# A chunked gated recurrence in a two-layer backbone step: forward and backward keys in one operand per level, the diagonal first, and the output-gate weighting behind the levels

## The chip, the cores and the metric

One core of a Trainium2 chip runs the whole step in one launch. The metric is the device time of an execution in microseconds (us). All arithmetic is in fp32. Engines are named as in the profile: PE (TensorE), DVE (VectorE), ACT (ScalarE), POOL (GpSimd), SP (the queue that issues the weight loads).

## The reference, cut to what matters

Two layers (L = 0, 1) over 384 tokens: 128 context tokens and 256 latent ones. Each layer mixes tokens (attention beside a bidirectional gated recurrence, joined by sigmoid gates) and then applies a mixture of 16 experts. The recurrence is the part that the change touches:

```
def hgrn_chunk_scan(q, k, v, log_f, s0):
    ...
        bcum = jnp.cumsum(gc, axis=2)
        o_inter = jnp.einsum('bhck,bhkv->bhcv', qc * jnp.exp(bcum), state)
        diff = bcum[:, :, :, None, :] - bcum[:, :, None, :, :]
        decay = jnp.exp(jnp.where(incl, diff, -jnp.inf))
        scores = jnp.einsum('bhtk,bhsk,bhtsk->bhts', qc, kc, decay)
        o_intra = jnp.einsum('bhts,bhsv->bhtv', scores, vc)
...
    o_f, s_f = hgrn_chunk_scan(q, k_f, v, lf_f, s0_f)
    o_b, s_b = hgrn_chunk_scan(flip(q), flip(k_b), flip(v), flip(lf_b), s0_b)
    o = o_f + flip(o_b)
    o = rms_norm(o, hnorm_w) * jax.nn.silu(heads(h_g.astype(F32), HGRN_V))
```

There are 4 heads of width 128. For a query t and a key s the score is a sum over channels of q, k and the decay between s and t: with the forward keys for s before t, with the backward keys for s after t, and with both on the diagonal.

## The kernel before

**Tiling.** Tokens lie in 3 tiles of 128; with 4 heads that makes 12 segments, and one operand of the recurrence is 128 channels x 1536 (12 x 128) values. `qh` holds q, `kg[0]` and `kg[1]` the forward and backward keys, `Cs[0]` and `Cs[1]` the running sums of the log forget gates (all in the buffer `gen`). The 128 x 128 score matrices of the 12 segments are gathered in `AT`.

**Levels.** A score matrix is filled level by level: with block size m = 64, 32, ..., 1 the pairs (s, t) that lie in the two halves of one block of 2m are computed, with the decay measured from the block's middle. The old order has 15 steps: each of the 7 levels once forward and once backward (step 2k and 2k+1), then the diagonal. For a step, POOL writes differences of `Cs` to the middle (L628, L629: two instructions of 128x768 each), ACT takes the exponential in place (L760, 128x1536), DVE multiplies one half of each block by keys and the other by queries (L1012, two instructions of 128x768) into `W[s % 2]`, and PE multiplies that operand with itself (L1470: 3 tiles x 4 heads, 128x128 each; the profile records two entries per fp32 matmul, so a step is 24). DVE copies each tile's result into `AT` where the step's mask is set (L1025, 3 instructions). `E[0]`, `E[1]`, `W[0]` lie in the buffer `ring`, `W[1]` in `modb`. The exponents use `E[s % 2]`, and POOL may write them for step s once DVE has made the operand of step s-2 (`lv_W`).

**Order of the work.** Each engine follows one hand-written program, and semaphores join them. PE writes projections into two banks in turn (`group` counts them). In the stretch at issue its program is: the 8 gate groups `ga` (L1410, 8 matmuls of 128x384 each), behind each one step of the levels (`LEV_AT`); in layer 0 then 8 modulation units `mod` 12 to 19 (L1364 and L1368, in pairs, each pair followed by two sums L1376), with a step behind each of the first 7; in layer 1 the last 7 steps with nothing between; then the branch groups `wba` (L1410 with 4 matmuls). Between these stand the key transposes `kd` (L1331), the chunk states (L1601) and the outputs (L1611 to L1616). ACT evacuates `ga` with a sigmoid (L815) and must load a function table on each change between sigmoid and exponential. For the modulation units it copies (L697, L702) and stores to memory (L706), and a pair may only be copied once the pair before it is stored.

**Behind the levels.** Four operands are exponentials of `Cs`, multiplied by `fin` (L1035): `W[1]` and `W[0]` by q for the outputs, `E[0]` and `E[1]` by the keys for the states. POOL makes two differences for them (L636, 128x1536). DVE copies the transposed keys (L1039), makes the states (L1136, L1141) and then norms the outputs. POOL multiplies the output gate `sg` by the norm's weights (L616, 3 instructions) ahead of its first difference.

**Weight loads.** SP loads 2 MB units into a ring of 4 slots in the order of use (L466). A unit's load is issued when the last group of the unit 4 places ahead of it is done: `mod` 15 when `ga` 7 is done, `mod` 16 to 19 when `mod` 12 to 15 are, and the branch weights `wba` when `mod` 16 is. The three expert weights (2 MB each) of an expert come through 6 slots behind `x_mid` and the last groups of the mixer.

## Time and profile before

| | us |
|---|---|
| median of 3 runs | 1647.63 |
| the runs | 1644.11 to 1647.88 |
| span of the profiled execution, first to last instruction | 1645.4 |
| PE busy | 1449.9 (88% of the span) |
| DVE busy | 533.4 (32%) |
| ACT busy | 340.7 (21%) |
| POOL busy | 212.7 (13%) |

The profile gives the execution's span; its time with what lies around it is not listed apart from the three runs. The span is 2.2 us below their median and within their range. PE's busy share is an average: in layer 0 the levels of the recurrence run from 275 to 381 us of the span, in layer 1 from 1061 to 1148 us. The experts fill 571 to 850 and 1325 to 1621 us.

### The profile page before, as it was taken

The numbers are of one execution on the slowest core, as the hardware profiler recorded it, in microseconds if no ns is written. First come the engines' busy times: TensorE is split into PE (matmuls) and PEld (weight loads), VectorE is DVE, ScalarE is ACT, GpSimd is POOL, SyncE is SP. The second block draws the span as 40 slices with busy tenths as digits, with TensorE's granted clock in tenths as the row PEclk, the third lists the DMA queues.
The fourth block names the chain that finished last, engine by engine and source line by source line (L and its number), as shares of the span: only waits on it lengthen the run. The fifth ranks groups of instructions, "written<-read, shape, count | busy, mean of one in ns | idle before, by whom it ended". The sixth has DMA issues, their size and how long they took to land.

```text
span 1645.4 us, 19345 instructions
## 1 busy us (share of the span) xinstructions
PE 1449.9 (88%) x7515; PEld 813.0 (49%) x7516; DVE 533.4 (32%) x1097; ACT 340.7 (21%) x499; POOL 212.7 (13%) x213
## 2 busy tenths in 40 slices
PE   4699998999999799989965999898999688999882
PEld 1365545766654354444423654577654344454441
DVE  1333323564212511121125353348511432111113
ACT  1105533532100201100101174354100100011100
POOL 2160004321100100000012500444100000000001
PEclk9799999999999799999987999999999889999997
DMA  9635552185333999996984412211223544799994
GB/s 347 237 106 186 186 215 80 52 292 182 128 107 113 397 349 396 397 344 248 399 305 141 155 54 70 84 52 52 90 103 111 221 158 169 278 398 394 398 394 184
DMA packets 157047, 352.48 MB, mean 214 GB/s; under 512 B 5880, under 2 KB 13128, under 8 KB 156992
## 3 DMA queue, kind: packets, MB, share of 16 engines
q1 hardware_dynamic: 138208, 314.48, 51.7%
q0 software_dynamic: 6576, 23.26, 3.9%
q10 hardware_dynamic: 12208, 13.98, 2.6%
q8 instruction: 38, 0.62, 0.2%
q14 instruction: 17, 0.14, 0.0%
HBM read 336.15 MB, written 15.55 MB: 214 GB/s over the span
## 4 chain that ended last, share of the span: by engine, by line
PE 74%; DVE 8%; SPq 7%; DMA 4%; issue 4%; ACT 1%; POOL 1%; DVEq 0%; ACTq 0%; POOLq 0%
PE pG L1410 22%; PE pS L1490 10%; PE pG L1402 8%; SPq L475 6%; PE pG L1505 5%; PE pG L1639 5%; PE pG L1498 4%; PE pS L1470 2%; PE pG L1364 2%; PE pX L1470 2%; DMA ring<-in_w_mod_dram 2%; PE pX L1331 2%; PE pX L1490 2%; DMA ring<-in_w_exp_up_dram 1%; PE pG L1376 1%
## 5 line engine op out<-in xcount | busy, mean ns | idle before, releaser
L1410 PE MATMUL pG<-hT,ring 128*128 128x384 f32 x896 | 299.7, 489 | 1.6 <-ACT gen L849 1.6
L1490 PE MATMUL pS<-ring,gen 128*64 128x256 f32 x2048 | 230.6, 381 | 12.2 <-DMA ring<-in_w_exp_up_dram 9.8
L1410 PEld LDWEIGHTS pG<-hT,ring 128*128 128x128 f32 x896 | 168.1, 191 | 115.6 <-issue 4.8
L1490 PEld LDWEIGHTS pS<-ring,gen 128*64 128x64 f32 x2048 | 149.5, 138 | 100.5 <-issue 20.1
L1402 PE MATMUL pG<-ring,hT 128*128 128x512 f32 (+1 forms) x384 | 150.0, 548 | 1.4 <-issue 0.7
L1505 PE MATMUL pG<-ring,gen 128*64 128x512 f32 x512 | 116.9, 598 | 5.1 <-DVE gen L1287 5.1
L1282 DVE TENSOR_TENSOR gen<-pS,gen 128x256 f32<-128x256 f32 x32 | 13.6, 424 | 314.8 <-PE pS L1490 314.8
L1402 PEld LDWEIGHTS pG<-ring,hT 128*128 128x128 f32 x384 | 72.6, 192 | 72.1 <-issue 67.7
L1498 PE MATMUL pG<-hrow,gen 128*64 128x512 f32 x408 | 96.0, 604 | 2.2 <-DVE gen L1182 1.5
L662 POOL DMA_INDIRECT gen<-y_scr,idx x12 | 11.6, 963 | 630.1 <-ACTq L899 627.0
L878 ACT COPY gen<-pG 128x512 f32<-128x512 f32 x32 | 18.8, 586 | 349.1 <-PE pG L1505 349.1
L1639 PE MATMUL pG<-ring,hrow 128*128 128x512 f32 x192 | 82.9, 593 | 2.5 <-DVE hrow L1167 2.5
L553 POOL TENSOR_TENSOR stat<-stat,half 128x8 f32<-128x8 f32 (+3 forms) x22 | 23.9, 1086 | 336.2 <-DVE stat L962 260.3
L1505 PEld LDWEIGHTS pG<-ring,gen 128*64 128x64 f32 x512 | 33.9, 136 | 67.5 <-issue 54.8
L1364 PE MATMUL pG<-ring,cst 128*32 128x512 f32 x384 | 52.6, 660 | 14.2 <-DMA ring<-in_w_mod_dram 14.2
L1639 PEld LDWEIGHTS pG<-ring,hrow 128*128 128x128 f32 x192 | 36.3, 190 | 48.7 <-issue 45.0
L1331 PE MATMUL pX<-const,gen 128*128 128x128 f32 x224 | 40.7, 291 | 22.3 <-DVE gen L1284 13.6
L1331 PEld LDWEIGHTS pX<-const,gen 128*128 128x128 f32 x224 | 23.2, 141 | 63.2 <-issue 26.0
L1498 PEld LDWEIGHTS pG<-hrow,gen 128*64 128x64 f32 x408 | 30.4, 140 | 48.2 <-issue 42.1
L628 POOL TENSOR_TENSOR ring<-gen 128x768 f32<-128x768 f32 x28 | 43.4, 1549 | 82.5 <-DVE modb L1012 41.9
L1331 PE MATMUL pS<-const,hrow 128*128 128x128 f32 x32 | 7.0, 391 | 47.0 <-DVE hrow L968 47.0
L1410 PE MATMUL pG<-modb,ring 128*128 128x384 f32 x128 | 46.7, 519 | 0.0
(269 smaller groups left out, 1713.4 us busy)
## 6 DMA issues: line engine op xcount, KB each, us to landing
ring<-in_w_exp_up_dram SPq DMA_DIRECT2D x32, 2048.0 KB, 20.7
ring<-in_w_exp_down_dram SPq DMA_DIRECT2D x32, 2048.0 KB, 19.3
ring<-in_w_exp_gate_dram SPq DMA_DIRECT2D x32, 2048.0 KB, 18.3
ring<-in_w_mod_dram SPq DMA_DIRECT2D x24, 2048.0 KB, 9.0
ring<-in_w_in_dram SPq DMA_DIRECT2D x20, 2048.0 KB, 7.8
modb<-mod_scr POOLq DMA_DIRECT2D x20, 512.0 KB, 8.9
y_scr<-gen ACTq DMA_DIRECT2D x72, 128.0 KB, 5.5
ring<-in_w_out_dram SPq DMA_DIRECT2D x4, 2048.0 KB, 10.2
```

What stands on the lines that cost most here:

```text
L475: return sp.dma_start(dst, src).then_inc(landed[s0 + part], 16)
L553: return pool.tensor_tensor(stat[:, stat0:stat0 + width], stat[:, stat0:stat0 + width], half[:, 0:width], ALU.pow).then_inc(done, 1)
L628: pool.tensor_tensor(out[:, :, :, 0, :], mid, base[:, :, :, 0, :], ALU.subtract)
L1331: return pe.transpose(out, in_, ident[0:n, 0:n])
L1364: pe.matmul(ps[32 * q:32 * q + 32, :], cst[:, 2 * q + k, :, :].rearrange("p c r -> p (c r)"), w[:, 2 * q + k, :], start=(k == 0), stop=(k ...
L1402: ins = pe.matmul(ps[:, 0:width], hT[:, k, t * P:(t + 1) * P], w[:, k, 0:width], start=(k == 0), stop=(k == KC - 1))
L1410: ins = pe.matmul(ps[:, 0:TOK], w[:, k, c0:c0 + P], src[:, k, :], start=(k == 0), stop=(k == nk - 1))
L1470: ins = pe.matmul(bank[2 + u % 4][:, P * h:P * (h + 1)], lhs, rhs, start=True, stop=True)
L1490: ins = pe.matmul(dst[64 * hf:64 * hf + 64, 0:256], x[:, k, :], w[:, k, 256 * hf:256 * (hf + 1)], start=(k == 0), stop=(k == KC - 1))
L1498: ins = pe.matmul(dst[64 * hf:64 * hf + 64, :], sel1[:, t, :], hrow[:, t, 512 * hf:512 * (hf + 1)], start=(t == 0), stop=(t == NT - 1))
L1505: ins = pe.matmul(dst[64 * hf:64 * hf + 64, :], x[:, k, :], w[:, k, 512 * hf:512 * (hf + 1)], start=(k == 0), stop=(k == 3))
L1639: ins = pe.matmul(ps, mergedT[:, k, t * P:(t + 1) * P], w[:, k, :], start=(k == 0), stop=(k == KC - 1))
```

## The change

The levels now take 8 steps. Step 0 is the diagonal; steps 1 to 7 are the levels, each once for both directions. Two operands are used per step, in the same four buffers: `LR[s % 2]`, a left and a right one, `E[0]` and `E[1]` for even steps, `W[0]` and `W[1]` for odd ones. The left one holds the keys with their decays (forward keys in the first half of each block, backward keys in the second), the right one the queries with theirs, so that one product yields the forward scores in one corner of a block and the backward scores in the other. POOL now makes four differences per step (two per operand), ACT two exponentials, DVE three products (two of 128x768 for the left operand, one of 128x1536 for the right). PE multiplies left by right, and the masks shrink from 15 to 8. POOL may write the operands of step s once PE has done step s-2 (`lv_mm`), since they are now what PE reads.

All 8 steps stand behind the 8 `ga` groups, in both layers; the modulation units of layer 0 follow without any. The exponentials for `fin` now come ahead of ACT's copies of the modulation units. `fin` 0 and 1 make the keys' operands, `fin` 2 and 3 the outputs', and these two stand behind `wba` 1 on DVE. `kd` 0 to 3 stand together behind `wba` 1 on PE, and DVE's copies of them also wait for the exponentials, which read the buffers that they overwrite. POOL's products of `sg` stand behind its differences.

```diff
-LEV_STEPS = 2 * NLEV + 1
-
-LEV_AT = {g: k for k, g in enumerate([("ga", j) for j in range(KC)] + [("mod", m) for m in range(MOD_LEV, MOD_LATE - 1)])}
+LEV_STEPS = NLEV + 1
...
+        LR = (E, W)
...
+                pool.wait_ge(at_outv, ATT_STEPS * (L + 1))
+                pool.wait_ge(C_ready, 2 * (L + 1))
+                for s in range(1, LEV_STEPS):
+                    m = 64 >> (s - 1)
+                    if s >= 2:
+                        pool.wait_ge(lv_mm, LEV_TILES * L + NT * (s - 1))
...
+                    left, right = (x.rearrange("p (s b u m) -> p s b u m", s=SEG, u=2, m=m) for x in LR[s % 2])
+                    pool.tensor_tensor(left[:, :, :, 0, :], mid[0], base[0][:, :, :, 0, :], ALU.subtract)
+                    pool.tensor_tensor(left[:, :, :, 1, :], base[1][:, :, :, 1, :], mid[1], ALU.subtract).then_inc(lv_D, 1)
+                    pool.tensor_tensor(right[:, :, :, 0, :], mid[1], base[1][:, :, :, 0, :], ALU.subtract)
+                    pool.tensor_tensor(right[:, :, :, 1, :], base[0][:, :, :, 1, :], mid[0], ALU.subtract).then_inc(lv_D, 1)
+
+                for d, dst in ((0, E[0]), (1, W[0])):
+                    pool.wait_ge(lv_mm, LEV_TILES * L + NT * (LEV_STEPS - 1 + d))
...
                 for t in range(NT):
                     pool.wait_ge(sg_mul, NT * L + t + 1)
...
             def lev(L, s):
-                if s < 2 * NLEV:
-                    act.wait_ge(lv_D, 2 * NLEV * L + s + 1)
-                    act.activation(E[s % 2], E[s % 2], ACT.Exp).then_inc(lv_E, 1)
+                if s < LEV_STEPS:
+                    for side in range(2):
+                        act.wait_ge(lv_D, 2 * (NLEV * L + s - 1) + side + 1)
+                        x = LR[s % 2][side]
+                        act.activation(x, x, ACT.Exp).then_inc(lv_E, 1)
...
-                    lev(L, LEV_AT[("ga", j)] + 2)
...
+                    lev(L, j + 1)
...
+                if s == 0:
+                    dve.wait_ge(C_ready, 2 * (L + 1))
+                    dve.tensor_tensor(LR[0][0], kg[0], kg[1], ALU.add).then_inc(lv_W, 1)
+                elif s < LEV_STEPS:
+                    m = 64 >> (s - 1)
+                    left, right = LR[s % 2]
+                    dve.wait_ge(lv_E, 2 * (NLEV * L + s - 1) + 1)
+                    for u in range(2):
+                        x, k = (v.rearrange("p (s b u m) -> p s b u m", s=SEG, u=2, m=m)[:, :, :, u, :]
+                                for v in (left, kg[u]))
+                        dve.tensor_tensor(x, x, k, ALU.mult)
+                    dve.wait_ge(lv_E, 2 * (NLEV * L + s - 1) + 2)
+                    dve.tensor_tensor(right, right, qh, ALU.mult).then_inc(lv_W, 1)
...
-                fin(L, 0, W[1], qh)
+                fin(L, 0, E[1], kg[1])
                 fin(L, 1, E[0], kg[0])
                 wba(L, 0)
...
+                for i in range(4):
+                    kd_evac(L, i)
                 wba(L, 1)
...
+                fin(L, 2, W[1], qh)
+                fin(L, 3, W[0], qh)
                 wba(L, 2)
```

**PE, layer 0, from the last `ga` group on.** 128x384 with x8 is a `ga` group, 128x128 a step, 32x512 x8 with 32x128 x4 a modulation unit, 32x512 x2 the two sums. Before:

```order
L1410 MATMUL pG<-hT,ring 128x384 x8
L1470 MATMUL pS<-modb 128x128 x4
L1470 MATMUL pX<-modb 128x128 x8
L1364 MATMUL pG<-ring,cst 32x512 x8
L1368 MATMUL pG<-brow,const 32x128 x4
L1470 MATMUL pS<-ring 128x128 x8
L1470 MATMUL pX<-ring 128x128 x4
L1364 MATMUL pG<-ring,cst 32x512 x8
L1368 MATMUL pG<-brow,const 32x128 x4
L1470 MATMUL pX<-modb 128x128 x4
L1470 MATMUL pS<-modb 128x128 x8
L1376 MATMUL pG<-modb,const 32x512 x2
```

and with the change:

```order
L1401 MATMUL pG<-hT,ring 128x384 x8
L1461 MATMUL pS<-modb,ring 128x128 x4
L1461 MATMUL pX<-modb,ring 128x128 x8
L1355 MATMUL pG<-ring,cst 32x512 x8
L1359 MATMUL pG<-brow,const 32x128 x4
L1355 MATMUL pG<-ring,cst 32x512 x8
L1359 MATMUL pG<-brow,const 32x128 x4
L1367 MATMUL pG<-modb,const 32x512 x2
```

The seven steps between the modulation units are gone, and the last step stands behind the last `ga` group.

**DVE, both layers, the first steps behind the last product of the output gate.** `modb` or `ring` ahead of the arrow is the operand being made. Before:

```order
L1115 TENSOR_TENSOR ring<-pG,ring 128x512
L1012 TENSOR_TENSOR ring<-gen,ring 128x12x64 x2
L1012 TENSOR_TENSOR modb<-gen,ring 128x12x64 x2
L1025 COPY_PREDICATED ring<-masks,pS 128x4x128 x2
L1025 COPY_PREDICATED ring<-masks,pX 128x4x128
L1012 TENSOR_TENSOR ring<-gen,ring 128x24x32 x2
```

and with the change:

```order
L1108 TENSOR_TENSOR ring<-pG,ring 128x512
L997 TENSOR_TENSOR ring<-gen 128x1536
L1005 TENSOR_TENSOR ring<-ring,gen 128x12x64 x2
L1007 TENSOR_TENSOR modb<-modb,gen 128x1536
L1017 COPY_PREDICATED ring<-masks,pS 128x4x128 x2
L1017 COPY_PREDICATED ring<-masks,pX 128x4x128
L1005 TENSOR_TENSOR ring<-ring,gen 128x24x32 x2
L1007 TENSOR_TENSOR ring<-ring,gen 128x1536
```

The first operand is now the sum of the two keys (L997), which needs no exponential; behind it every step has three products and three masked copies.

**PE behind the levels.** L1331 (now L1322) with x8 are two of the four `kd`, L1601 (now L1584) the states, L1611 (now L1595) the outputs. Before:

```order
L1410 MATMUL pG<-modb,ring 128x384 x4
L1331 MATMUL pS<-const,ring 128x128 x8
L1410 MATMUL pG<-modb,ring 128x384 x4
L1331 MATMUL pX<-const,ring 128x128 x8
L1410 MATMUL pG<-modb,ring 128x384 x4
L1601 MATMUL pS<-gen 128x128 x4
```

and with the change:

```order
L1401 MATMUL pG<-modb,ring 128x384 x8
L1322 MATMUL pS<-const,ring 128x128 x8
L1322 MATMUL pX<-const,ring 128x128 x8
L1401 MATMUL pG<-modb,ring 128x384 x4
L1584 MATMUL pS<-gen 128x128 x4
```

Two branch groups now stand ahead of the first transposes.

## Rows read from the trace of the kernel before

**Rows 1.** the page: chain of waits by engine, share of the span

```profile
PE 74%; DVE 8%; SPq 7%; DMA 4%; issue 4%; ACT 1%; POOL 1%; DVEq 0%; ACTq 0%; POOLq 0%
```

**Rows 2.** chain of waits, layer 0, gate groups and steps (start, us, what)

```profile
289.00 5.16 PE pG L1410 x16
294.17 1.78 PE pX L1470 x16
295.95 0.89 PE pS L1470 x8
296.84 5.16 PE pG L1410 x16
...
333.37 0.89 PE pS L1470 x8
```

**Rows 3.** timeline, layer 0, first step (start, us, instruction, [idle before, releaser])

```profile
265.80 0.69 DVE L1115 TENSOR_TENSOR ring<-pG,ring 128x512 f32<-128x512 f32 x1 [7.25 <-ACT ring L807]
266.57 1.27 POOL L616 TENSOR_TENSOR ring<-ring,hnw 128x512 f32<-128x512 f32 x1 [6.87 <-DVE ring L1115]
...
272.11 1.48 POOL L629 TENSOR_TENSOR ring<-gen 128x768 f32<-128x768 f32 x1
272.33 2.94 DVE L1012 TENSOR_TENSOR ring<-gen,ring 128x768 f32<-128x768 f32 x2 [5.84 <-ACT ring L760]
...
275.33 3.79 PE L1470 MATMUL pS<-ring 128*128 128x128 f32 x16 [5.10 <-DVE ring L1012]
...
276.42 0.49 ACT L815 ACTIVATE hrow<-pG 128x384 f32<-128x384 f32 x1
```

**Rows 4.** lines of the levels: count, ns (min/median/max), starts, form

```profile
L628 POOL TENSOR_TENSOR ring<-gen x28: 1466/1503/2076, 267.8 to 1133.5; 128x768 f32<-128x768 f32 x28
...
L1012 DVE TENSOR_TENSOR ring<-gen,ring x28: 936/951/2090, 272.3 to 1137.2; 128x768 f32<-128x768 f32 x28
...
L1014 DVE TENSOR_TENSOR ring<-gen x2: 1731/1736/1741, 368.2 to 1143.4; 128x1536 f32<-128x1536 f32 x2
...
L1025 DVE COPY_PREDICATED ring<-masks,pS x46: 712/731/746, 278.2 to 1148.2; 128x512 f32<-128x512 uint8 x46
...
L760 ACT ACTIVATE ring<-ring x28: 1467/1485/1490, 270.7 to 1136.5; 128x1536 f32<-128x1536 f32 x28
...
L760 ACT ACT_TABLE_LOAD  x18: 1283/1283/1283, 265.7 to 1119.2; - x18
```

**Rows 5.** chain of waits, layer 1: its first level

```profile
1060.90 3.78 PE pS L1470 x16
```

**Rows 6.** stretches: us, PE PEld DVE ACT POOL busy, clock, DMA share, GB/s

```profile
355.00:365.00 10.00, 10.00 (x80) 6.01 (x73) 5.95 (x8) 3.12 (x4) 0.00 (x0) 1.00 0.98 360
...
1121.00:1148.00 27.00, 20.50 (x172) 19.40 (x171) 26.84 (x33) 8.54 (x8) 11.43 (x7) 1.00 0.17 70
```

**Rows 7.** timeline, layer 1, last levels and what follows them

```profile
1128.72 2.05 PE L1470 MATMUL pX<-ring 128*128 128x128 f32 x16 [1.78 <-DVE ring L1012]
...
1148.01 2.75 PE L1410 MATMUL pG<-modb,ring 128*128 128x384 f32 x8
...
1148.25 2.75 POOL L636 TENSOR_TENSOR ring<-gen 128x1536 f32<-128x1536 f32 x1 [0.25 <-PE pS L1470]
...
1154.33 1.18 PE L1331 MATMUL pS<-const,ring 128*128 128x128 f32 x8 [3.58 <-DVE ring L1035]
...
1155.31 4.39 PE L1410 MATMUL pG<-modb,ring 128*128 128x384 f32 x8
...
1169.15 1.28 PE L1611 MATMUL pX<-gen,ring 128*128 128x128 f32 x10
```

**Rows 8.** DMA issues of 255 to 400 us: count, KB each, median us to landing

```profile
ring<-in_w_mod_dram SPq DMA_DIRECT2D x7, 2048.0 KB, 8.5
```

**Rows 9.** timeline, layer 0: first branch group, first recurrence output

```profile
384.87 2.85 PE L1410 MATMUL pG<-modb,ring 128*128 128x384 f32 x8
...
407.59 1.28 PE L1611 MATMUL pX<-gen,ring 128*128 128x128 f32 x10
```

More of the change, by code:

```diff
@@ L611, in _ @@
                     last.then_inc(qk_ready, 1)
+                pool.wait_ge(at_outv, ATT_STEPS * (L + 1))
[4 more added lines that the diff above has]
+                        pool.wait_ge(lv_mm, LEV_TILES * L + NT * (s - 1))
+                    base, mid = [], []
+                    for d in range(2):
+                        base.append(Cs[d][:, :, 1 - d:129 - d].rearrange("p s (b u m) -> p s b u m", u=2, m=m))
+                        mids = Cs[d][:, :, m:m + 128 - 2 * m + 1:2 * m] if m < 64 else Cs[d][:, :, 64:65]
+                        mid.append(mids.unsqueeze(3).broadcast_to([P, SEG, 64 // m, m]))
+                    left, right = (x.rearrange("p (s b u m) -> p s b u m", s=SEG, u=2, m=m) for x in LR[s % 2])
[5 more added lines that the diff above has]
+                    pool.wait_ge(lv_mm, LEV_TILES * L + NT * (LEV_STEPS - 1 + d))
+                    end = Cs[d][:, :, 128:129].broadcast_to([P, SEG, P])
+                    pool.tensor_tensor(dst.rearrange("p (s t) -> p s t", s=SEG), end, Cs[d][:, :, 1 - d:129 - d],
+                                       ALU.subtract).then_inc(fin_D, 1)
                 for t in range(NT):
@@ L815, in _ @@
                     act.activation(mergedT[:, j, :], ps[:, 0:TOK], ACT.Sigmoid).then_inc(ga_ready, 1)
[L816 to L830 removed]
+                    lev(L, j + 1)
+                act.wait_ge(lv_mm, LEV_TILES * L + NT * (LEV_STEPS - 1))
+                act.activation(E[1].rearrange("p (s t) -> p s t", s=SEG), Cs[1][:, :, 0:128], ACT.Exp)
                 for d in range(2):
@@ L835, in _ @@
                 act.activation(E[0], E[0], ACT.Exp).then_inc(fin_E, 1)
+                act.wait_ge(lv_mm, LEV_TILES * (L + 1))
+                act.activation(W[1].rearrange("p (s t) -> p s t", s=SEG), Cs[0][:, :, 1:129], ACT.Exp).then_inc(fin_E, 1)
                 act.wait_ge(fin_D, 2 * L + 2)
                 act.activation(W[0], W[0], ACT.Exp).then_inc(fin_E, 1)
-                act.wait_ge(lv_W, LEV_STEPS * (L + 1))
-                act.activation(E[1].rearrange("p (s t) -> p s t", s=SEG), Cs[1][:, :, 0:128], ACT.Exp).then_inc(fin_E, 1)
+                if L == 0:
+                    for m in range(MOD_LEV, MOD_LATE, 2):
+                        mod_copy(m)
+                        mod_copy(m + 1)
+                        mod_store(m)
+                        mod_store(m + 1)
                 act.wait_ge(st_ready, 4 * L + 2)
@@ L1574, in _ @@
                     cols(L, ("ga", j), w, P * (j % 4), hT, KC)
-                    lev(L, LEV_AT[("ga", j)])
+                    lev(L, j)
                 if L == 0:
                     for m in range(MOD_LEV, MOD_LATE, 2):
-                        for i in range(2):
-                            mod(m + i)
-                            if ("mod", m + i) in LEV_AT:
-                                lev(L, LEV_AT[("mod", m + i)])
+                        mod(m)
+                        mod(m + 1)
                         mod_sum(m)
                         mod_sum(m + 1)
-                else:
-                    for s in range(KC, LEV_STEPS):
-                        lev(L, s)
                 w = unit_in(L, ("wba", 0))
@@ L1589, in _ @@
                     cols(L, ("wba", j), w, P * j, attnT, 4)
-                    if j == 0:
-                        kd(L, 0)
-                        kd(L, 1)
                     if j == 1:
-                        kd(L, 2)
-                        kd(L, 3)
+                        for i in range(4):
+                            kd(L, i)
                     if j == 2:
```

68 lines of the change are left out of this document (7 added, 61 removed).

## The prediction

> **What bounds the kernel now.** I read the page first: PE is busy for 88% of the span, as the table of the page's shares has it, and the chain of waits lies on PE for 74% [rows 1]. So the question at each place is whether PE waits, and for whom. The levels are then read in the chain of layer 0 [rows 2]: a gate group of 5.16 us and a step of 1.78 + 0.89 = 2.67 us follow each other without a gap, 7.84 us a pair. There PE is the bound, and the other engines' work on a step is hidden. It is not hidden in two places. Before the first step PE is idle for 5.10 us, and then its clock is low: 16 entries take 3.79 us [rows 3]. In layer 1 the last seven steps have no gate group beside them: between 1121 and 1148 us PE is busy for 20.50 of 27.00 us, DVE for 26.84 [rows 6].
>
> **What it removes on PE.** 15 steps become 8: 7 steps of 2.67 us, 18.7 us of PE work per layer and 37.4 in all, if PE were the only bound. POOL, ACT and DVE keep their work on the levels (7 steps with twice as much each instead of 14), save that DVE makes 7 x 3 = 21 fewer masked copies of 0.73 us per layer [rows 4], all off the path.
>
> **A step from now on.** The first four POOL differences of the levels start from 267.8 to 272.11 us, one every 1.44 [rows 3, 4]: 5.8 us in all for a step. ACT needs two exponentials of 1.48 and, around the gate sigmoid of 0.49, two table loads of 1.28 [rows 3, 4]: 6.0 us. DVE needs two products of 0.95 us, one of 1.74 (the sum at L1014 has its shape) and three copies of 0.73: 5.8 us [rows 4]. Each is under PE's 7.84. But POOL and DVE hold each other up. A POOL difference of 1.48 us starts at 272.11 and ends at 273.59; two DVE products, from 272.33 on, take 2.94 instead of 1.9 us, and for 1.26 of these POOL was still busy [rows 3]. The longest of L1012 is 2.09 us and of L628 2.08, where 0.95 and 1.50 are the medians [rows 4], so it goes both ways, and the masked copies, at most 0.75, are spared. The two thus take turns: 5.8 + 2 x 0.95 + 1.74 = **9.4 us** per step, more than PE's 7.84. With steps 1 to 7 that is what sets the pace, and PE waits some 1.6 us in each. The Trainium skill, GPSIMD Engine Reference, section 3.1 on elementwise work, gives about 2.6 cycles per element for a two-input GpSimd operation, 1.66 us for 768 elements; by that the pace would be 10.3 us and the kernel some 11 us slower than I forecast. The trace has 1.47 to 1.50, and I keep that.
>
> **Both layers, start to last step.** I count in the times of layer 0 before. The last gate product of DVE ends at 266.5 [rows 3], and the new first operand is a sum of 1.74 us with no exponential, ready at 268.3. `ga` 0 ends at 275.33 - 5.10 = 270.2. So step 0 runs at once, to 272.9: the 5.1 us and the low clock behind it go. What is late next is step 1. POOL has done it early: moving the output-gate products behind the levels lets it in, and it was idle for 6.87 us before the last of them [rows 3]. But ACT takes its exponentials only behind the sigmoid of `ga` 0: 270.2 + 0.5 + 1.3 + 2 x 1.5 = 275. POOL's four differences for step 2 start at 272.9, and DVE's three products, from 273.6 on, take turns with them, to 281. `ga` 1 ended at 278.1: PE waits 2.9 us. Six more steps at 9.4 bring step 7 to 337.3 and its end to **340.0**. In layer 1 the first step begins at 1060.90 instead of 275.33 [rows 5, 3], 785.6 later, and the stretch is otherwise the same: its last step ended at 1148.0 [rows 7], which is 362.4 in layer 0's times. **Layer 1 gains 22.4 us** here.
>
> **Layer 0, the modulation units.** From the first step behind `ga` 7 to `wba` 0 went 333.37 to 384.87 [rows 2, 9], 51.5 us; less eight steps of 2.67 that is 30.1 us for the units and their sums. Now their weights bound them. With the change the loads are still issued behind groups: `mod` 15 when `ga` 7 ends (335.7), landing 8.5 us later [rows 8] at 344.2, and `mod` 16, 17, 18, 19 and `wba` behind units that are done by then. In the old order the queue moved 360 GB/s when it was full [rows 6], 5.8 us per 2 MB, and five more loads end at 373.2. So `wba` 0 starts there instead of at 384.87 [rows 9]: **11.7 us**. (If the units took their 30.1 us of PE time behind step 7, it would be 370.) ACT copies `mod` 12 only behind the last exponentials, some 4 us late, which the loads cover; without them it would cost 2 to 3 us.
>
> **Behind the levels.** In layer 1 the first outputs came 21.1 us behind the last step (1148.0 to 1169.15), with 3.58 us idle ahead of the transposes and a branch group of 4.39 us at the low clock instead of 2.75 [rows 7]. Now POOL's second difference (2.75 us [rows 7]) starts at the end of step 7, the first `fin` waits for it, POOL's `sg` products of 1.27 us [rows 3] take a turn between the two `fin` of 1.74, and both operands are ready 7.6 us behind the last step. Two branch groups fill 5.4 of them. Then four transposes (0.9 each, as 8 entries of a step [rows 2]), a branch group (2.7), four states (3.6), a branch group (2.7): 20.2 us. `fin` 2 and 3 run beside the states. **1 us gained.** In layer 0 all of `fin` 0 and 1 is done behind the modulation units: 4 branch groups and 7.2 us, 18 instead of 22.7 us (384.87 to 407.59 [rows 9]): **4.7 us gained.**
>
> **The sum.** 22.4 + 1 in layer 1, 11.7 + 4.7 in layer 0: 39.8 us. What follows starts on groups and semaphores that come earlier by as much, the expert loads too. The smaller mask load and cast lie beside other work; I give them nothing. 1645.4 - 39.8 = 1605.6 for the span, and the median of the runs is 2.2 above it: **1607.8 us**. Unknown are the turns of POOL and DVE. At best they cost nothing and PE's 7.84 returns: 6 x 1.56 + 2 = 11.4 us less per layer, 1585. At worst I take 0.4 us more per step for handing over, and PE's clock low for one group per layer (4.39 against 2.75 [rows 7]): 5 + 3 = 8 us more, 1616.
>
> **The rivals.**
> - *Turns cost nothing, PE is the bound*: 1585 us. For it: behind the gate groups of layer 0 they were hidden [rows 2]. Against: there POOL and DVE needed only 4.8 of 7.84 us. 8%.
> - *The two operand pairs do not overlap.* POOL is let in by PE's end of step s-2, where it was let in by DVE before. If a step's chain ran alone (5.8 POOL, 1.5 ACT, 1.7 DVE, 2.7 PE, 11.7 us), 12 steps would cost 2.3 us more each: 1635. Against: with two pairs that chain is shared by two steps. 9%.
> - *The modulation units keep their old length* of 51.5 us behind the last gate group, through ACT's copies and stores: from 335.7 on that ends at 387.2, 14 us later than I forecast, 1622. For it: the copies of a pair wait for the stores of the pair before. Against: the steps stood between them, and PE did not wait. 8%.
> - *PE falls to the low clock and stays there: slower.* If the waits in each step held PE at 1.2 GHz, a group and a step would take 2 x 7.84 = 15.7 us, 12 times 6.3 more: 1683. It is slower than now from 9.4 + 39.8 / 12 = 12.7 us per step on. Against: in layer 1 PE waited 1.78 us before a step [rows 7] in a stretch where the granted clock was 1.00, with PE busy 76% of the time [rows 6]; the new waits are 1.6 in 9.4. The Trainium skill, TensorE: Matmul & The Clock Gate, section HAM oscillation, warns of just this, a loop whose waits send the clock down each time; the trace does not bear it out at waits of this length. 3%.
> - *No gain arrives*, since the experts' loads are bound elsewhere: 1648. Against: those loads start on events that move with PE. 2%.
>
> **How the numbers follow.** My forecast has 70%, at 1607.8, between 1594 and 1618. The range of 1584 to 1626 takes in the first and third rival and leaves out the others, 14%, and a little of the first's tail. About 0.3% (5 us) is what a measurement can tell from no change. Faster by more: all but the last two, 0.95. The same: 0.02. Slower: 0.03.
>
> **What would show it.** PE starts step 0 within 0.1 us of `ga` 0; DVE products of 768 at 2 us and more many times over, steps 1 to 7 at 9.4 us; `wba` 0 in layer 0 some 33 us behind step 7, with DMA full; 20 us from the last step to the outputs in layer 1, without a low clock. I am wrong if a step takes 7.8 or 11.7 us, or if the granted clock in the gate stretch is well below 0.95.

## The result, and the profile after

| | before | after |
|---|---|---|
| median | 1645.87 us (4 runs, 1643.84 to 1647.88) | 1605.52 us (4 runs, 1598.92 to 1606.07) |
| ratio, 95% interval | | 0.9748 [0.9732, 0.9764] |
| profiled execution: its time, its span | -, 1645.4 | 1598.92, 1597.1 |

The change takes 40 us off, and 39.8 were forecast. The profiled execution is the fastest of the four, 6.6 us below their median, so a second trace of the same kernel (after_again, 1603.29 us) stands beside it below. The page's chain of waits by engine, beside [rows 1], says that PE still carries it, with DVE a little more than before:

```profile
PE 71%; DVE 10%; SPq 7%; DMA 6%; ACT 3%; issue 2%; POOL 0%; DVEq 0%; ACTq 0%; POOLq 0%
```

**The gate stretch of layer 0** in the timeline of PE (start, us, instruction, [idle before, releaser]); it answers to [rows 2, 3]:

```profile
260.34 5.32 PE L1401 MATMUL pG<-hT,ring 128*128 128x384 f32 x16
265.50 1.95 PE L1461 MATMUL pS<-gen,ring 128*128 128x128 f32 x16
...
275.91 1.16 PE L1461 MATMUL pX<-modb,ring 128*128 128x128 f32 x8 [2.41 <-DVE modb L1007]
...
283.85 1.95 PE L1461 MATMUL pX<-ring 128*128 128x128 f32 x16
...
294.44 1.16 PE L1461 MATMUL pS<-modb,ring 128*128 128x128 f32 x8 [2.58 <-DVE modb L1007]
...
314.35 1.16 PE L1461 MATMUL pX<-modb,ring 128*128 128x128 f32 x8 [2.33 <-DVE modb L1007]
...
331.38 1.16 PE L1461 MATMUL pS<-modb,ring 128*128 128x128 f32 x8 [1.07 <-DVE modb L1007]
```

Step 0 follows its gate group at once, where 5.10 us were empty and 16 entries took 3.79 us [rows 3]. Step 1 waits 2.41 us (2.9 were forecast). After step 1 the picture is not the forecast's: PE waits only ahead of the odd steps, whose right operand is in `modb`; step 2 at 283.85 has no wait. On average a step takes (331.38 - 275.91) / 6 = 9.25 us, and 9.4 were forecast.

**What a wait ahead of an odd step consists of** stands in the chain of waits of the same stretch (start, us, what). Gate group 2 ends at 284.03 and step 3 starts at 294.44:

```profile
284.05 0.49 ACT hrow L813
...
284.56 1.28 ACT L760
...
285.86 1.50 ACT ring L760
...
287.38 1.41 DVE ring L1005
...
289.06 2.27 DVE ring L1005
291.33 3.07 DVE modb L1007
294.40 0.04 issue
294.44 1.16 PE pS L1461 x8
```

That is the sigmoid of the gate group, the table, the left exponential and then DVE's three products: 10.4 us in all, beside 2.67 + 5.16 = 7.84 us of PE work (step 2 and gate group 3). The difference is the wait of 2.58. The products are slow in it, as forecast: by their lines (count, ns min/median/max, starts, form) those of `modb` take 3.03 us instead of 1.74 [rows 4]. POOL's third differences for the even steps are slow as well, 2.22 instead of 1.50:

```profile
L1007 DVE TENSOR_TENSOR modb<-modb,gen x8: 1745/3033/3136, 272.8 to 1099.7; 128x1536 f32<-128x1536 f32 x8
...
L624 POOL TENSOR_TENSOR ring<-gen x6: 2176/2216/2297, 272.0 to 1079.0; 128x768 f32<-128x768 f32 x6
...
L1017 DVE COPY_PREDICATED ring<-masks,pS x24: 705/717/741, 275.8 to 1103.2; 128x512 f32<-128x512 uint8 x24
```

The masked copies keep their 0.72. Ahead of step 7 POOL has one difference beside these products instead of four, DVE's last product takes 1.75 us, and PE waits only 1.07.

An even step does not wait, although its products can be slow too. The timeline of DVE and POOL, step 2 (first row) and step 4:

```profile
279.36 3.07 DVE L1007 TENSOR_TENSOR ring<-ring,gen 128x1536 f32<-128x1536 f32 x1
...
296.16 1.80 DVE L1005 TENSOR_TENSOR ring<-ring,gen 128x768 f32<-128x768 f32 x2
...
297.89 1.74 DVE L1007 TENSOR_TENSOR ring<-ring,gen 128x1536 f32<-128x1536 f32 x1
...
299.04 1.97 POOL L622 TENSOR_TENSOR ring<-gen 128x768 f32<-128x768 f32 x1 [3.22 <-PE pX L1461]
```

Step 2's last product takes 3.07 us and ends at 282.4, 8.9 us behind the end of gate group 1 (273.5). PE, which has its wait of 2.41 us, step 1 and gate group 2 in between, needs it at 283.85. So it is the wait ahead of the odd step that gives the even one its lead. At step 4, where step 3 ran at the low clock (below), POOL is let in late and sits idle for 3.22 us; DVE makes all three products alone in 3.5 us. One step in two pays.

**The clock.** Stretches of after (us, busy of PE, PEld, DVE, ACT and POOL, granted clock, DMA share, GB/s):

```profile
284.00:294.00 10.00, 7.86 (x41) 5.39 (x39) 6.91 (x4) 7.99 (x8) 10.00 (x6) 1.00 0.10 16
294.00:299.00 5.00, 4.56 (x25) 4.56 (x26) 5.00 (x7) 3.95 (x3) 1.82 (x1) 0.66 1.02 386
...
1063.00:1067.00 4.00, 4.00 (x22) 4.00 (x23) 4.00 (x6) 3.29 (x3) 1.30 (x1) 0.57 1.05 403
...
1083.00:1087.00 4.00, 4.00 (x24) 4.00 (x25) 4.00 (x6) 3.59 (x3) 1.11 (x1) 0.63 0.00 0
```

Three times behind a wait of this kind the clock is at its lower level for part of a step. The even step then starts 9.6 us behind the odd one instead of 8.0, 1.6 us each, 4.8 in all. It comes back at once: by 299 it is 1.00.

The second trace has the same waits and more falls. In layer 0 the clock falls behind all three of 2.41, 2.58 and 2.33 us (first and last of them):

```profile
276.50:280.80 4.30, 4.30 (x25) 4.30 (x25) 4.30 (x6) 3.68 (x3) 1.30 (x1) 0.63 0.00 0
...
316.40:321.00 4.60, 4.54 (x25) 4.54 (x26) 4.60 (x7) 3.82 (x3) 1.33 (x1) 0.63 0.01 4
```

In layer 1 it falls at the same two places as in the first. So five falls, some 8 us, stand in an execution near the median, and three in the fastest: a step of layer 0 takes (335.11 - 276.50) / 6 = 9.77 us there instead of 9.25. In layer 1 it takes 9.52 in both.

**Behind the levels** (windows, then the timeline of PE in layer 0 and in layer 1; they answer to [rows 6, 7, 9]):

```profile
334.00:368.00 34.00, 29.04 (x212) 12.90 (x211) 7.50 (x4) 13.26 (x19) 9.47 (x4) 1.00 1.01 377
```

```profile
362.41 1.92 PE L1355 MATMUL pG<-ring,cst 128*32 128x512 f32 x16 [2.59 <-DMA ring<-in_w_mod_dram]
...
367.91 5.43 PE L1401 MATMUL pG<-modb,ring 128*128 128x384 f32 x16 [0.94 <-DMA ring<-in_w_br_attn_dram]
...
383.66 1.28 PE L1595 MATMUL pX<-gen,ring 128*128 128x128 f32 x10
```

```profile
1104.27 5.33 PE L1401 MATMUL pG<-modb,ring 128*128 128x384 f32 x16
1111.66 1.09 PE L1322 MATMUL pS<-const,ring 128*128 128x128 f32 x8 [2.07 <-DVE ring L1027]
1112.59 1.04 PE L1322 MATMUL pX<-const,ring 128*128 128x128 f32 x8
...
1122.20 1.28 PE L1595 MATMUL pX<-gen,ring 128*128 128x128 f32 x10
```

In layer 0 the DMA queues are full for 34 us at 377 GB/s, and the first branch group starts at 367.9, 33.6 us behind step 7's end (334.3); 33.2 were forecast.

**The accounts**, from the start of gate group 0 in each layer:

| us | before | after | gained | forecast |
|---|---|---|---|---|
| layer 0, to its first outputs | 264.9 to 407.6: 142.7 | 260.3 to 383.7: 123.3 | 19.4 | 16.4 |
| layer 1, to the last step's end | 1050.5 to 1148.2: 97.7 | 1028.8 to 1104.4: 75.6 | 22.1 | 22.4 |
| layer 1, from there to the outputs | 21.0 | 17.8 | 3.2 | 1 |

These rows sum to 44.6 us. The two spans differ by 48.3: before gate group 0 of layer 0 the profiled execution of after is 4.6 us shorter (260.3 against 264.9), from layer 0's outputs to layer 1's gate group 2.3 us longer, and 1.4 lie behind. The 4.6 us are not the change: the second trace has 260.9 there, and a variant below that differs only among the gate groups 264.3. By the second trace the three rows gain 16.5, 22.1 and 3.2 us, 41.8 in all, and the stretch between the layers is 3.6 us longer. The 3 us less in layer 0 are its two more falls of the clock.

### The profile page after: what moved, and what is told of

The parts are those of the page before. It is cut to its first block, busy times and chain, and to the rows that moved or that the text cites. A ratio compares the mean times of both kernels' runs of the same rounds, so it can differ in the third digit from the quotient of the medians.

```text
span 1597.1 us, 18517 instructions
## 1 busy us (share of the span) xinstructions
PE 1401.8 (88%) x7179; PEld 768.5 (48%) x7180; DVE 519.8 (33%) x1041; ACT 335.0 (21%) x495; POOL 240.2 (15%) x213
## 4 chain that ended last, share of the span: by engine, by line
PE 71%; DVE 10%; SPq 7%; DMA 6%; ACT 3%; issue 2%; POOL 0%; DVEq 0%; ACTq 0%; POOLq 0%
PE pG L1401 21%; PE pS L1481 10%; PE pG L1393 9%; SPq L472 6%; PE pG L1496 5%; PE pG L1623 5%; PE pG L1489 4%; DMA ring<-in_w_mod_dram 2%; PE pX L1322 2%; PE pX L1481 2%; DVE ring L1005 2%; PE pG L1355 2%; DMA ring<-in_w_exp_up_dram 1%; DVE modb L1007 1%; PE pX L1447 1%
## 5 line engine op out<-in xcount | busy, mean ns | idle before, releaser
L622 POOL TENSOR_TENSOR ring<-gen 128x768 f32<-128x768 f32 x14 | 23.4, 1675 | 294.2 <-DVE modb L990 259.4
L1322 PE MATMUL pX<-const,gen 128*128 128x128 f32 x224 | 40.7, 291 | 22.3 <-DVE gen L1275 13.6
L1005 DVE TENSOR_TENSOR ring<-ring,gen 128x768 f32<-128x768 f32 x28 | 41.8, 1532 | 38.2 <-ACT ring L760 38.2
L1322 PEld LDWEIGHTS pX<-const,gen 128*128 128x128 f32 x224 | 23.2, 141 | 63.1 <-issue 26.0
L1322 PE MATMUL pS<-const,hrow 128*128 128x128 f32 x32 | 6.8, 385 | 46.6 <-DVE hrow L961 46.6
```

The costliest lines, as they stand in the source:

```text
L622: pool.tensor_tensor(left[:, :, :, 0, :], mid[0], base[0][:, :, :, 0, :], ALU.subtract)
L1005: dve.tensor_tensor(x, x, k, ALU.mult)
L1322: return pe.transpose(out, in_, ident[0:n, 0:n])
```

## The experiments

Each is timed against the kernel before on the same chip. The sets ran on different chips, so across them the ratios compare better than the times.

**after_again: the changed kernel once more.**

> The changed kernel again, as the mark for the runs beside it. Both theories: 1605 us, some 0.975 of before. A second trace also shows whether the 4.4 us by which the first stretch (up to the first gate group) was shorter in the profile after belong to the change: if they do, the first gate group of layer 0 starts at 260.5 us again; if it is how TensorE's clock happened to come up at the start, it may start near 265.

1603.29 us (1600.71 to 1609.1), 0.9749 [0.9728, 0.977]. The same waits in layer 0: 2.41, 2.58, 2.33 and 1.07 us. The waits are a property of the kernel; the falls of the clock behind them are not the same in every execution (five here, three in the first trace). The first stretch is short again (260.9), so by this trace alone it could have been the change's; a9 and a12 below show otherwise. The variants can be held against some 1603 to 1606 us.

**a3_more_pe: more PE work in each step.**

```diff
-                        ins = pe.matmul(bank[2 + u % 4][:, P * h:P * (h + 1)], lhs, rhs, start=True, stop=True)
+                        for _ in range(2 if t == 0 else 1):
+                            ins = pe.matmul(bank[2 + u % 4][:, P * h:P * (h + 1)], lhs, rhs, start=True, stop=True)
```

> In each step the four products of the first token tile are made twice, 0.9 us more PE work per step. Theory (turns set the pace): the waits of about 2.4 us ahead of every second step take it in; only step 0 and what stands behind step 7 see it, 2 to 4 us more in all. Rival (PE is the bound): 8 steps in 2 layers, 14 us more.

1602.43 us (1600.82 to 1606.87), 0.9744 [0.9724, 0.9765]: no slower. The waits take it up (timeline of PE):

```profile
276.73 2.05 PE L1462 MATMUL pX<-modb,ring 128*128 128x128 f32 x16 [0.77 <-DVE modb L1007]
...
295.32 2.05 PE L1462 MATMUL pS<-modb,ring 128*128 128x128 f32 x16 [0.86 <-DVE modb L1007]
```

The two odd steps are 18.6 us apart, as in after (18.5). PE does not set the pace. But the time stands still only because gains cancel a cost. The clock does not fall once:

```profile
262.00:336.00 74.00, 70.92 (x385) 52.45 (x383) 56.02 (x46) 46.79 (x42) 52.91 (x25) 1.00 0.21 72
```

And the stretch from gate group 2's end to step 3, where PE is not the bound, shrinks from 10.4 to 9.6 us while PE's part grows by 0.9: POOL is let in 0.9 us later, and the two left products take 3.18 us instead of 3.96. From gate group 0's start to the start of what follows the last step it is 74.0 us in each layer, where the changed kernel takes 73.9 and 75.5 in the first trace and 77.1 and 75.5 in the second.

**a2_short_right_diff: less POOL work.** POOL makes a twelfth of the right differences, and the right exponentials ignore them, so the queries' decays are left out of the scores.

```diff
-                    pool.tensor_tensor(right[:, :, :, 0, :], mid[1], base[1][:, :, :, 0, :], ALU.subtract)
+                    pool.tensor_tensor(right[:, 0:1, :, 0, :], mid[1][:, 0:1], base[1][:, 0:1, :, 0, :], ALU.subtract)
...
-                        act.activation(x, x, ACT.Exp).then_inc(lv_E, 1)
+                        act.activation(x, x, ACT.Exp, scale=float(1 - side)).then_inc(lv_E, 1)
```

> POOL's two differences for the right operand cover 1 of 12 segments, and the right exponential is scaled by 0, so the scores are not the reference's; all waits and all other work stay. Theory (POOL and DVE take turns, and their sum sets the pace): the sum falls from 9.4 to about 6.8 us per step, under PE's 7.84, so steps 1 to 7 come every 7.8 us and the kernel takes 16 to 20 us less, 1585 to 1589. Rival (ACT's exponentials behind the gate sigmoid set the pace): the pace stays near 9.2 us, above 1600.

1589.58 us (1588.69 to 1594.32), 0.9669 [0.9649, 0.9689]. Steps 1 to 7 are (327.1 - 275.2) / 6 = 8.65 us apart, and PE still waits 1.21, 1.31, 1.16 and 1.07 us ahead of the odd ones. The clock holds (1.00 over both gate stretches), which is a part of the gain. No piece of POOL stands in the chain of waits of the changed kernel's gate stretch, so its work costs time through DVE's products, as the theory says; but with that much of it gone PE's 7.84 should have come back, and did not.

**a9_exp_first: ACT's exponentials ahead of the gate sigmoid.**

```diff
+                    lev(L, j + 1)
                     ps = sync_group(L, ("ga", j))
                     act.activation(mergedT[:, j, :], ps[:, 0:TOK], ACT.Sigmoid).then_inc(ga_ready, 1)
-                    lev(L, j + 1)
```

> ACT takes the exponentials of step j + 1 ahead of the sigmoid of gate group j instead of behind it; nothing else moves. Theory (turns set the pace): step 1 no longer waits (2.4 us less per layer), the pace of steps 2 to 7 stays at 9.2 us: 1600 to 1604. Rival (ACT's place behind the sigmoid sets the pace): all waits ahead of the steps go, 7.8 us a step, 10 us less per layer, 1585.

1589.78 us (1586.4 to 1590.82), 0.9654 [0.9636, 0.9672]: my theory had 1600 to 1604 and fell, and the rival's 1585, with no wait left, was not reached either. POOL and DVE do the same work, yet 14 us are gone. In the timeline of PE and of DVE:

```profile
295.24 4.22 DVE L1005 TENSOR_TENSOR ring<-ring,gen 128x768 f32<-128x768 f32 x2
...
299.38 3.06 DVE L1007 TENSOR_TENSOR ring<-ring,gen 128x1536 f32<-128x1536 f32 x1
...
302.49 2.05 PE L1461 MATMUL pS<-ring 128*128 128x128 f32 x16 [0.85 <-DVE ring L1007]
...
311.39 1.16 PE L1461 MATMUL pX<-modb,ring 128*128 128x128 f32 x8 [0.79 <-DVE modb L1007]
```

The waits are under a microsecond, now ahead of even and odd steps alike, and the clock holds (1.00 from 1028 to 1094). From 293.5 to 320.0 three steps take 26.5 us, 8.84 each. So in the changed kernel the wait is not the sum of the turns but a chain: ACT's 3.3 us behind the gate group, then products slowed by the turns. Not all 14 us are the chain's, though: the changed kernel's three to five falls of the clock among the gate groups, 5 to 8 us, are gone with the waits behind which they came, while one appears in layer 1's tail, which takes 19.5 us instead of 17.8.

**a5_right_exp_psum and a10_exp_first_psum: less work in turns, with ACT behind and ahead of the sigmoid.** Two thirds of each right exponential go to PSUM, and DVE's product reads them there. ACT also waits for DVE's operand of the step before, since both use the same banks.

```diff
-                        act.activation(x, x, ACT.Exp).then_inc(lv_E, 1)
+                    for i in range(2):
+                        act.activation(bank[6 + i], right[:, 512 * (i + 1):512 * (i + 2)], ACT.Exp)
+                    act.activation(right[:, 0:512], right[:, 0:512], ACT.Exp).then_inc(lv_E, 1)
...
-                    dve.tensor_tensor(right, right, qh, ALU.mult).then_inc(lv_W, 1)
+                    for i in range(3):
+                        c = slice(512 * i, 512 * (i + 1))
+                        ins = dve.tensor_tensor(right[:, c], bank[5 + i] if i else right[:, c], qh[:, c], ALU.mult)
+                    ins.then_inc(lv_W, 1)
```

> The change, with columns 512 to 1535 of each right exponential written to two PSUM banks, so that DVE's product reads them from there; ACT has one or two more instructions, the arithmetic is the same. Theory of the turns (POOL and DVE exclude each other when both read two operands from SBUF; a DVE instruction with one operand in PSUM is spared, as the masked copies are): the need of the shared turn falls from 9.4 to 8.2 us a step, 12 steps in all: 1605 - 14 = 1591, with 1587 to 1597. Rival (ACT's place behind the gate sigmoid alone sets the pace, as the 14 us that the exponentials first gave could mean): no gain, 1603 to 1607, or worse by the extra ACT instructions, 1610.

> The same with PSUM, and ACT's exponentials of a step also ahead of the gate sigmoid, the version that took 1589.8 us at 8.57 us a step. Theory (turns are what is left in that version): the step falls to PE's 7.84 us, 12 x 0.73 = 9 us less, 1579 to 1583. Rival (what is left there is the chain POOL, ACT, DVE, PE through two operand pairs): no gain or a small one, 1587 to 1591, since the chain is as long as before or longer by ACT's extra instructions.

a5: 1604.44 us (1598.44 to 1608.53), 0.975 [0.973, 0.9771], nothing gained. a10: **1576.06 us** (1570.66 to 1580.59), 0.9579 [0.9557, 0.9602], 14 us less than a9 by the times and 12 by the ratios. The same edit is worth nothing with ACT behind the sigmoid and 12 to 14 us with ACT ahead. Timeline of a5, step 3:

```profile
288.36 3.96 DVE L1009 TENSOR_TENSOR ring<-ring,gen 128x768 f32<-128x768 f32 x2 [2.96 <-ACT ring L759]
...
292.24 2.07 DVE L1013 TENSOR_TENSOR modb<-modb,gen 128x512 f32<-128x512 f32 x1
...
294.23 1.28 DVE L1013 TENSOR_TENSOR modb<-pX,gen 128x512 f32<-128x512 f32 x2
...
295.56 1.16 PE L1468 MATMUL pS<-modb,ring 128*128 128x128 f32 x8 [2.72 <-DVE modb L1013]
```

The third on SBUF is a third as large and still takes 2.07 us, since it waits for POOL's running difference (291.46 to 293.76); the whole product took 3.07. With the two from PSUM, 1.28 for both and not held up, nothing is won. In a10 the same third takes 0.69 us with POOL idle, some 1.9 beside a POOL difference of 1.5 us, and 3.10 beside the one of 2.75 us (317.05). So what a DVE product with both operands in SBUF pays goes by the POOL instruction beside it, not by its own size. In a10 the same rows stand off the chain, which is PE alone (chain of waits; then a stretch of it):

```profile
290.28 0.89 PE pS L1468 x8
291.17 1.79 PE pX L1468 x16
292.96 5.16 PE pG L1408 x16
298.12 1.78 PE pS L1468 x16
```

```profile
261.00:324.00 63.00, 63.00 (x321) 45.68 (x320) 56.22 (x60) 46.27 (x53) 41.82 (x25) 1.00 0.21 71
```

All eight steps stand 7.84 us apart. PE is the bound, and PE waits for nothing in the gate stretch. The time lies 3 us under the 1579 to 1583 that were expected, and its range reaches into them.

**a13_pool_halves: the same POOL work in pieces of half the size.**

```diff
-                    pool.tensor_tensor(left[:, :, :, 0, :], mid[0], base[0][:, :, :, 0, :], ALU.subtract)
...
+                        for g in (slice(0, SEG // 2), slice(SEG // 2, SEG)):
+                            pool.tensor_tensor(x[:, g, :, 0, :], mid[i][:, g], base[i][:, g, :, 0, :], ALU.subtract)
```

> The change with each of POOL's four differences of a step made in two instructions of half the size (128x384); the work is the same but for the fixed cost of four more instructions. Theory (a DVE product waits for the POOL instruction that is running, so what the turn costs is set by the size of POOL's pieces, not by the sum of the work): the two left products of an odd step take 3.1 us instead of 3.9, the right one 2.5 instead of 3.1, and the wait of PE ahead of an odd step falls from 2.4 by 1.4 us, where that chain sets it: 1605 - 10 = 1595, with 1592 to 1599. Rival (only the sum of both engines' work counts, 9.4 us a step, a little more with four more instructions): 1605 to 1610.

1602.07 us (1595.36 to 1607.19), 0.9736 [0.9708, 0.9764]. Neither the 1592 to 1599 of the theory nor the rival's 1605 to 1610 was met. DVE's products are shorter than my theory had them in the stretch shown (2.49 us for the two left ones, 1.76 for the right one), but POOL now pays (timeline, then the stretch 285 to 325):

```profile
286.66 2.49 DVE L1007 TENSOR_TENSOR ring<-ring,gen 128x768 f32<-128x768 f32 x2 [1.19 <-ACT ring L762]
286.71 3.16 POOL L626 TENSOR_TENSOR modb<-gen 128x384 f32<-128x384 f32 x2
...
289.90 1.48 ACT L762 ACTIVATE modb<-modb 128x1536 f32<-128x1536 f32 x1 [3.27 <-POOL modb L626]
```

```profile
285.00:325.00 40.00, 34.83 (x172) 25.30 (x171) 26.92 (x25) 24.41 (x22) 39.83 (x36) 0.96 0.15 53
```

Two half differences of 0.8 take 3.16 us, POOL is busy or held for 39.83 of 40 us, and ACT waits for it. Steps come 9.5 us apart. Here cutting one side's pieces moved the waiting to the other.

**b1_diag_first: the kernel before, with the diagonal first alone.** Besides the operand's turn in `W[s % 2]`, POOL's products of `sg` stand behind the levels.

```diff
             def lev(L, s):
-                if s < 2 * NLEV:
+                s -= 1
+                if 0 <= s < 2 * NLEV:
...
-                    if s < 2 * NLEV:
-                        m, d = 64 >> (s // 2), s % 2
+                    if s > 0:
+                        m, d = 64 >> ((s - 1) // 2), (s - 1) % 2
```

> The kernel before with one part of the change: its 15 steps stay, but the diagonal is step 0, and POOL's products of sg stand behind the levels. Theory (the empty time ahead of the first step and the low clock behind it are a part of the gain that has nothing to do with joining the directions): 5.10 us of waiting and 3.79 - 2.67 = 1.1 us of low clock go in each layer, 12.4 us in all: 1646.1 - 12.4 = 1633.7, with 1631 to 1638. Rival (the wait only moves to step 1, as it did in the change, where 2.4 us came back): 1638 to 1640. Rival (layer 1's last seven steps are bound by DVE and take back what came early there): 1640, with layer 0 alone faster.

1634.36 us (1628.41 to 1636.65), 0.9926 [0.9909, 0.9943]: 11 us, where 12.4 were expected. No PE wait is left in layer 0's stretch: from 265 to 372 PE is busy for 107.00 of 107 us. In layer 1 the levels end 90.9 us behind the gate group's start instead of 97.7, but 2 us come back behind them (23.0 instead of 21.0 to the outputs): the first transposes now wait 4.66 us, where they waited 3.58 [rows 7]. So about a quarter of the change's 40 us is the diagonal's place, and has nothing to do with joining the directions. My 12.4 rests on a slip that happens to fit: it sets 16 entries at the low clock (3.79 us) against a whole step of 24 (2.67). From 275.33 [rows 3] to the next gate group at 280.61 the step took 5.28 us, so the low clock cost 2.6, not 1.1. By the traces layer 0 gains 9.4 us to its outputs and layer 1 4.8, and the stretch between them, which the edit leaves alone, is 4.0 longer; why stays open.

**a4_sg_ahead: POOL's `sg` products ahead of the levels again.**

```diff
+                for t in range(NT):
+                    pool.wait_ge(sg_mul, NT * L + t + 1)
...
                 pool.wait_ge(at_outv, ATT_STEPS * (L + 1))
                 pool.wait_ge(C_ready, 2 * (L + 1))
```

> The change with POOL's three products of sg ahead of the levels again. Theory: POOL's four differences for step 1 start only behind the last product, some 2.9 us behind the start of gate group 0, take turns with DVE's sum and end about 9 to 10 us behind it; the right exponential follows, and step 1 comes 2 to 3 us later in each layer than now. Behind the levels of layer 1 POOL's products no longer stand beside the fin operands, worth at most 1 us: 1605 + 4 = 1609, with 1606 to 1612. Rival (the place is worth nothing, since ACT's exponentials wait for the sigmoid of gate group 0 in any case): 1603 to 1606.

1604.11 us (1601.3 to 1607.47), 0.9747 [0.9729, 0.9764]: no difference. Step 1 waits 2.98 us instead of 2.41, and the outputs of layer 1 follow the last step by 16.7 instead of 17.8 us. Both effects are there and cancel. The move that let POOL in early is worth nothing here, as ACT comes behind `ga` 0 anyhow; with the exponentials first it wasn't tried.

**a8_kd_early: two transposes back behind the first branch group.**

```diff
-                    if j == 1:
-                        for i in range(4):
-                            kd(L, i)
+                    if j == 0:
+                        kd(L, 0)
+                        kd(L, 1)
+                    if j == 1:
+                        kd(L, 2)
+                        kd(L, 3)
```

> The change with the key transposes 0 and 1 back behind the first branch group, as before the change. Theory: nothing in layer 0, where the operands are long ready; in layer 1 PE has 2.75 us of work instead of 5.4 until they are ready 7.2 us behind the last step, so it waits about 4.7 us instead of 2.1: 2.6 us, and up to 1.6 more if the clock falls for the next branch group: 1606 to 1610 against 1605. Rival (the order of the two is worth nothing, as DVE sets the end of this stretch): the same wait in sum, outputs 17.9 us behind the last step as now.

1609.93 us (1605.57 to 1611.33), 0.9782 [0.9767, 0.9797]. In layer 1 (timeline of PE):

```profile
1119.21 1.97 PE L1324 MATMUL pS<-const,ring 128*128 128x128 f32 x8 [4.65 <-DVE ring L1027]
1120.97 3.52 PE L1403 MATMUL pG<-modb,ring 128*128 128x384 f32 x8
```

The wait is 4.65 us instead of 2.07, and the clock falls behind it (1.97 and 3.52 instead of 1.09 and 2.75). The outputs follow the last step by 21.9 instead of 17.8 us: 4 us, about as large as the difference of the times.

**a6_mods_between and a12_exp_first_psum_mods: four modulation units of layer 0 between the gate groups.**

```diff
                     cols(L, ("ga", j), w, P * (j % 4), hT, KC)
+                    if L == 0 and j in AHEAD:
+                        mod(AHEAD[j])
                     lev(L, j)
```

Their weight loads and ACT's copies and stores move with them.

> The change with four of the eight modulation units of layer 0 moved: units 12, 13 and 15 between the gate groups 1, 3, 5 and their steps, unit 14 behind step 3. The work is the same. Theory: PE waits 2.4 to 2.6 us ahead of each odd step for DVE's operand, and a unit of 3.8 us put there fills the wait of steps 1, 3 and 5, 7.4 us in all; the waits for weights in the stretch behind the levels (33.6 us there for 30.1 of work) shrink too, by up to 3.5: 1605 - 7 to 11 = 1594 to 1598. Rival (ACT's copies and stores of these units, which now stand between the exponentials, make the operands later by as much): 1602 to 1607. Rival (the 2 MB loads alone bound layer 0 from the gate groups to the first branch group, whatever the order): 1605.

> The version that took 1576.1 us (exponentials ahead of the gate sigmoid, two thirds of the right ones in PSUM), with the modulation units moved as well. Theory: PE has no wait left among the gate groups there (7.84 us a step), so the units fill nothing, and only the waits for weights behind the levels can shrink, at most 33.6 - 30.1 = 3.5 us: 1572 to 1576. Rival (the units are worth the same as in the change alone, 7 to 11 us): 1565 to 1569. Rival (ACT, now with three exponential instructions, two table loads, a sigmoid, a copy and a store in a step, falls behind PE): 1578 or more.

a6: 1592.72 us (1586.83 to 1595.07), 0.967 [0.9651, 0.9688], 11 to 13 us less. a12: 1576.46 us (1575.84 to 1578.33), 0.9582 [0.9569, 0.9595], the same as a10. PE work moved into the waits is worth time while there are waits, and nothing once they are gone. In a12 the loads take the rest: PE waits at 360.62 for the branch weights,

```profile
360.62 5.43 PE L1431 MATMUL pG<-modb,ring 128*128 128x384 f32 x16 [2.06 <-DMA ring<-in_w_br_attn_dram]
```

and layer 0 takes 111.9 us from the gate group to the outputs, with 112.3 in a10. In layer 0 a6 takes 115.1 us for 123.3 in the first trace of the changed kernel and 126.1 in the second, 8.2 to 11.0 less. So the gain is found in layer 0. A part of it is the clock: from 261 to 345 us it holds at 1.00, and the changed kernel's one to three falls there are gone. In layer 1, where a6 changes nothing, two remain.

## Why the prediction was right

**The time and the sum.** 1605.5 us against 1607.8. The terms: layer 1 to the last step 22.1 (22.4), layer 0 in all 19.4 (16.4), layer 1's tail 3.2 (1). By the second trace layer 0 gave 16.5. The sum comes closer than its terms deserve: these rows give 41.8 to 44.6 us instead of 39.8, and other stretches, which the change leaves alone, take back or add a few us from one execution to the next.

**The start of the levels.** Step 0 at once, no low clock, a wait ahead of step 1: as forecast (2.41 for 2.9 us), and b1 shows the diagonal's part alone.

**The step's pace** is right in size (9.25 to 9.77 for 9.4 us) and half right in its cause. The step of the prediction that failed is "the two thus take turns: ... 9.4 us per step", taken as a sum that bounds every step, with "some 1.6 us" of waiting in each. DVE and POOL do take turns, and a2 and a10 show that it costs time. But the changed kernel doesn't run at the bound of that sum, which a9 puts at 8.84 us. It runs on a chain of 10.4 us from a gate group's end through ACT's sigmoid, table and exponential to three slowed products; every second step pays 2.3 to 2.6 us, the next one gets its lead from that wait. Without falls of the clock this would be some 9.0 us a step (an estimate: 9.25 in layer 0 less one fall of 1.6 over six steps). The falls, three in one trace and five in the other, add 5 to 8 us, which the sum put at nothing; only the upper end of the range counted 3 of them. That a sum of 9.4 and this chain with the clock's part give nearly the same pace is luck. ACT's 6.0 us per step were counted and put aside because they are under 7.84; it is their place behind the gate group, not their sum, that costs.

**The rivals.** *Turns cost nothing* fell (a2, a3). *The modulation units keep their old length* fell (33.6 us, not 51.5), and so did *no gain arrives*. *The operand pairs do not overlap* fell: an odd step starts 9.1 to 10.6 us behind the even one before it, an even one 8.0, or 9.6 with the clock low, never 11.7. *PE falls to the low clock* was seen for 4 to 5 us at a time, three times in one trace and five in the other, and never stayed. Of the Trainium skill's HAM oscillation (TensorE: Matmul & The Clock Gate) the traces thus agree with the fall behind a wait, but not in every turn of the loop. My argument against it, a wait of 1.78 us at full clock [rows 7], held for waits of that length, and the actual ones were 2.3 to 2.6. The price of a difference by the Trainium skill's GPSIMD Engine Reference (section 3.1, an estimate of 1.66 us by it) is not borne out: undisturbed ones take 1.47 to 1.50.

**The modulation units** are bound by their loads as forecast (33.6 for 33.2 us), although the units' PE work of 30.1 us is only 3.5 less. ACT's late copies are covered but for two waits of PE, 0.15 and 0.86 us.

**Behind the levels** a term was mis-sized: four transposes at 0.9 us each, 3.6. They take 0.93 for two, 1.8 in all; a row of 8 entries holds two of them, not one. That is 1.8 of the 2.2 to 2.4 us by which both tails are shorter than forecast (15.8 for 18, 17.8 for 20.2). The wait for the operands ends 7.2 us behind the last step; 7.6 were forecast. a8 shows that the place of the transposes is worth 4 us.

## What to carry to other kernels

When a change joins steps, follow one operand from the instruction that releases it to the one that waits, through every engine's program order: sums per engine, each under the bound, did not show a wait that came from one engine's instructions standing behind an unrelated one. Where two engines take turns, a piece of work pays for the other side's piece, so a smaller piece of its own saved little here, and halving the other side's moved the wait over. Removing one of two causes in series may show nothing, as with the exponentials in PSUM; try the pair before giving either up. Here the order of ACT's instructions and the use of PSUM together make the changed kernel 27 to 29 us faster still, 1576 us against 1645 of before. And look whether the clock falls behind a wait before pricing it: a wait of 2.4 us cost up to 4, and a change that shortens it may gain both.

## What was not expected of the hardware

- The granted clock fell behind waits of 2.3 to 2.6 us at some places (0.57 to 0.66 over 4 to 5 us) and not at others of the same length, and the same place can differ between two executions of one kernel: in layer 0 it fell behind the wait of step 3 alone in one, behind those of steps 1, 3 and 5 in the other. With waits of 0.9 us at most it stayed at 1.00 (a9). Behind one of 2.07 us in layer 1's tail a branch group took 4.05 us in a9 and 2.75 in the changed kernel. What decides between the equal ones stays open.
- A DVE product of 128x512 takes 0.68 us with one operand in PSUM while POOL is at work (0.674 to 0.684 in all 56 of a5 and a10), and up to 2.07 (a5) and 3.11 (a10) with both in SBUF.
- Before any of the changed code PE reaches the same point at 260.3 to 265.3 us in different profiled executions. The granted clock at the start goes with it: from 60 to 80 us it is 0.66 to 0.68 in the four that come at 264.3 or later (before, b1, a9, a12) and 0.83 to 0.91 in the ten others. That is 0.3% of the time, of the 0.2 to 0.7% by which the runs of one kernel differ.
